# A two-layer attention and expert kernel: the first section of a group runs whole in the fourth head, and the last group's second section is cut in two

## The reference

```python
g = jax.nn.sigmoid(merge_g).reshape(B, S, N_BRANCHES, D)
mix = g[:, :, 0] * (o_sb @ w_br_sb) + g[:, :, 1] * (o_nsa @ w_br_nsa) + g[:, :, 2] * (o_moba @ w_br_moba)
x = layer_norm(DEEPNORM_ALPHA * x + mix @ w_out, ln1_g, ln1_b)
return layer_norm(DEEPNORM_ALPHA * x + peer_ffn(x, ...), ln2_g, ln2_b)

# peer_ffn, for a block of 128 tokens
v1, i1 = lax.top_k(s1, PEER_TOPK)            # scores of x @ w_q against two sets of 128 keys
v2, i2 = lax.top_k(s2, PEER_TOPK)
...
g = jax.nn.softmax(top, axis=-1)
act = jax.nn.gelu(jnp.einsum('thkd,td->thk', u_tab[idx], xb).astype(jnp.float32))
return jnp.einsum('thk,thkd->td', (g * act).astype(v_tab.dtype), v_tab[idx])
```

## Time and profile before

| | us |
|---|---|
| median of 3 runs | 2804.93 (2803.51 to 2806.49) |
| span of the profiled execution | 2819.9 |
| PE busy | 2453.4 (87%) |
| DVE busy | 1942.6 (69%) |
| POOL busy | 1233.1 (44%) |
| DMA moved | 776.98 MB, mean 276 GB/s |

### The profile page before, as it was taken

The page is one execution under the profiler, slowest core; times in us unless marked ns, Lnnn a source line. Parts: engine busy times, 40 slices in busy tenths (PEclk is TensorE's granted clock), DMA queues, the critical chain, the costliest instruction groups (busy, mean ns, idle before and its releaser), DMA issues.

```text
span 2819.9 us, 30185 instructions
## 1 busy us (share of the span) xinstructions
PE 2453.4 (87%) x10632; PEld 1484.2 (53%) x10632; DVE 1942.6 (69%) x4009; ACT 786.9 (28%) x1563; POOL 1233.1 (44%) x1028
## 2 busy tenths in 40 slices
PE   8998998998999989899988887999989999987126
PEld 4764476575445357657654465476445347644012
DVE  0122245588988875667886887587998886687875
ACT  2243222213344332321342212212445333301001
POOL 0000023354565432434553655164656352656775
PEclk9998999999989999999997998999999899999569
DMA  4323258787888776977896999787889685998998
GB/s 144 105 73 100 90 188 337 273 290 253 304 283 302 266 251 224 379 286 270 323 359 246 338 375 350 272 297 255 298 297 330 221 308 200 394 366 317 362 373 320
DMA packets 224183, 776.98 MB, mean 276 GB/s; under 512 B 23200, under 2 KB 39712, under 8 KB 219552
## 3 DMA queue, kind: packets, MB, share of 16 engines
q0 software_dynamic: 147456, 536.94, 52.1%
q1 hardware_dynamic: 73696, 227.80, 22.6%
q10 hardware_dynamic: 2880, 10.31, 0.9%
HBM read 766.56 MB, written 8.39 MB: 275 GB/s over the span
## 4 chain that ended last, share of the span: by engine, by line
PE 57%; DVE 15%; DMA 9%; issue 8%; POOL 7%; ACT 3%; another core or an unknown queue 0%; DVEq 0%; ACTq 0%; SPq 0%
PE ps L1056 14%; PE ps L931 7%; PE ps L900 6%; PE ps L984 6%; PE ps L1089 5%; POOL rows L840 4%; DVE x L1535 4%; DMA rows<-in_table_u,idx 4%; PE ps L886 3%; DMA rows<-in_table_v,idx 3%; PE ps L1124 3%; DVE rows L1520 2%; PE ps L1150 2%; DMA wring<-in_merge 2%; PE ps L993 2%
## 5 line engine op out<-in xcount | busy, mean ns | idle before, releaser
L840 POOL DMA_INDIRECT rows<-in_table_u,idx x462 | 565.2, 1223 | 1021.3 <-DVE idx L1643 506.7
L1056 PE MATMUL ps<-xT,wring 128*128 128x256 f32 x3072 | 768.1, 399 | 56.5 <-DMA wring<-in_merge 24.6
L840 POOL DMA_INDIRECT rows<-in_table_v,idx x434 | 526.5, 1213 | 490.5 <-DVE x L1535 362.4
L1056 PEld LDWEIGHTS ps<-xT,wring 128*128 128x128 f32 x3072 | 586.2, 197 | 245.4 <-issue 90.4
L1520 DVE CUSTOM_DVE_ANT_0 rows<-rows,x 128x1024 f32<-128x1024 f32 x462 | 555.0, 1223 | 120.0 <-DMA rows<-in_table_u,idx 114.3
L1535 DVE SCALAR_TENSOR_TENSOR x<-rows,wts,x 128x1024 f32<-128x1024 f32 x413 | 529.8, 1283 | 65.6 <-DMA rows<-in_table_v,idx 43.6
L1089 PE MATMUL ps<-KA,QA 33*128 33x512 f32 (+7 forms) x576 | 253.7, 537 | 26.5 <-DVE part_m L1777 12.9
L1389 ACT ACTIVATE scratch<-scratch,negm 128x640 f32<-128x640 f32 (+7 forms) x192 | 143.5, 747 | 475.3 <-DVE negm L1777 464.6
L900 PE MATMUL ps<-wring,G 128*128 128x512 f32 x384 | 184.8, 617 | 9.7 <-DVE G L1678 6.3
L1777 DVE CUSTOM_DVE_ANT_0 scratch<-ps,cst 128x128 f32<-128x128 f32 (+3 forms) x192 | 86.9, 454 | 143.0 <-PE ps L1089 140.3
L886 PE MATMUL ps<-oT,wring 128*128 128x256 f32 x384 | 126.0, 464 | 53.0 <-DVE G L1673 35.1
(11 more groups left out here) (209 smaller groups left out, 2951.4 us busy)
## 6 DMA issues: line engine op xcount, KB each, us to landing
wring<-in_merge SPq DMA_DIRECT2D x216, 512.0 KB
wring<-in_w_out_h SPq DMA_DIRECT2D x48, 512.0 KB
wring<-in_w_query SPq DMA_DIRECT2D x32, 512.0 KB
G<-in_w_query SPq DMA_DIRECT2D x12, 1024.0 KB, 8.5
G<-in_x SPq DMA_DIRECT2D x16, 512.0 KB, 4.6
G<-in_ln SPq DMA_DIRECT2D x8, 1024.0 KB, 6.8
G<-x_mid SPq DMA_DIRECT2D x16, 512.0 KB, 5.4
rows<-in_table_u,idx POOLq DMA_INDIRECT x462
```

The costliest lines, as they stand in the source:

```text
L840: pool.indirect_dma_start(row_slot(n), None, tab_u if table == "u" else tab_v, bass.IndirectOffsetOnAxis(ap=idx[:, GT * (g % 2) + t, e:e + ...
L1056: mm = pe.matmul(gate_bank(p)[:, SW * n:SW * (n + 1)], w[:, lo:lo + P], xT[:, kc, SW * (p // HALF_GATES):SW * (p // HALF_GATES + 1)], star ...
```

## The change

`SECTIONS` becomes a list of (group, tiles). The first section of every group now runs from `tanh` to `route` inside phase 3, without gates among it; gates 12 to 23 all stand in phase 4. In the last group the second section becomes two: `MIDDLE` (tile 2), placed in phase 4 behind the gates, and `LAST` (tile 3), alone behind the pass. A section of one tile has 6 merge pieces, 2 outs and 2 queries, and its merge and query matmuls move 128 columns and not 256. Both load their own weights, all through the ring.

```diff
+SECTIONS = [(g, (0, 1) if s == 0 else (2, 3)) for g in range(NG) for s in range(NS)][:-1] + [(NG - 1, (2,)), (NG - 1, (3,))]
+MIDDLE, LAST = len(SECTIONS) - 2, len(SECTIONS) - 1
 def early_section():
-    first = [("tanh", 0, 0, 0.0)] + [("gate", 0, (HALF_GATES, part), 0.0) for part in range(PARTS)]
-    first += gate_steps(HALF_GATES + 1) + [("merge", 0, k, 1.5) for k in range(12)] + section_outs(0) + gate_steps(HALF_GATES + 2)
-    second = [("norm", 0, 1, 0.0)] + gate_steps(HALF_GATES + 3)
-    second += [("turn", 0, k, 1.5) for k in range(2 * ST)] + sum([query_steps(0, k) for k in range(4)], [])
-    second += [("match", 0, k, 1.2) for k in range(2 * ST)] + [("route", 0, tt, 0.5) for tt in range(ST)]
-    return first, second + sum([gate_steps(p) for p in range(HALF_GATES + 4, GATES)], [])
+    first = [("tanh", 0, 0, 0.0)] + [("merge", 0, k, 1.5) for k in range(12)] + section_outs(0)
+    first += [("norm", 0, 1, 0.0)] + [("turn", 0, k, 1.5) for k in range(2 * ST)] + sum([query_steps(0, k) for k in range(4)], [])
+    return first + [("match", 0, k, 1.2) for k in range(2 * ST)] + [("route", 0, tt, 0.5) for tt in range(ST)]
+def tile_section(s):
+    steps = [("merge", s, k, 1.5) for k in range(6)] + section_outs(s, 1) + [("norm", s, 0, 0.0)]
+    steps += [("turn", s, k, 1.5) for k in range(2)] + sum([query_steps(s, k) for k in range(2)], [])
+    return steps + [("match", s, k, 1.2) for k in range(2)] + [("route", s, 0, 0.5)]
...
+        elif phase == 3:
+            streams.append((0.0, early_section(), 0.97))
         else:
-            streams.append((0.0, early_section()[phase - 3], 0.95))
+            own = [("tanh", MIDDLE - NS * g, 0, 0.0)] + tile_section(MIDDLE - NS * g) if g == NG - 1 else []
+            streams.append((0.0, sum([gate_steps(p) for p in range(HALF_GATES, GATES)], []) + own, 0.97))
...
-            streams.append((0.0, row_steps(phase, GT * half + phase), 0.85))
+            streams.append((0.0, row_steps(phase, GT * half + phase), 0.85 if phase < 3 else 0.5))
...
-BLOCKS = [(sec, table, ST * s + tt) for sec, (g, s) in enumerate(SECTIONS)
-          for table, tt in (("u", 0), ("u", 1), ("v", 0), ("v", 1))]
+BLOCKS = [(sec, table, t) for sec, (g, tiles) in enumerate(SECTIONS) for table in ("u", "v") for t in tiles]
...
+            def ring_section(sec):
+                for b in (2, 1, 0):
+                    load("br", sec, b)
+                if sec != MIDDLE:
+                    residual(sec)
+                for n in range(4):
+                    load("o", sec, n)
+                if sec != MIDDLE:
+                    norm_rows(sec)
+                for n in range(4, 8):
+                    load("o", sec, n)
+                for n in range(8):
+                    load("q", sec, n)
                 load("k", sec)
...
-            sp.wait_ge(oT_copied, GT * NG)
-            late_section(NS * NG - 1)
+            ring_section(MIDDLE)
+            ring_section(LAST)
```

More of the change, by code:

```diff
@@ L215, in head_steps @@
     route = [("route", -1, tt, 0.5) for tt in range(ST)]
-    steps = [("tanh", -1, 0, 0.0)]
     if g == NG:
-        steps += merge + outs + turn[0:2] + norm + turn[2:4]
-        return steps + sum(query, []) + match + route
-    steps += turns[0:2]
+        return tile_section(LAST - NS * NG)
+    steps = [("tanh", -1, 0, 0.0)] + turns[0:2]
     for n in range(6):
@@ L361, in expert_shares @@
                 late = s == 0
-            now += (.78 if kind in HEAD_KINDS or s < 0 else 1.12 if not late else 1.0 if g % 2 else 1.1) * pe
+            now += (.78 if kind in HEAD_KINDS or s < 0 else 1.12 if not late else 1.05) * pe
             if kind in ("tanh", "turn") and s < 0:
-                ahead = 1.0 if g == NG else TIGHT_AHEAD if kind == "tanh" else EXPERT_AHEAD
+                ahead = TIGHT_AHEAD if kind == "tanh" else EXPERT_AHEAD
+            if g >= NG - 1 and sec in (MIDDLE, LAST) and kind in ("merge", "turn"):
+                ahead = 0.5 if kind == "merge" or g == NG else EXPERT_AHEAD
             while nxt < ready:
@@ L683, in used @@
                     else:
-                        sp.wait_ge(done, 2 * (twos * n + m) + 2)
+                        sp.wait_ge(done, before + each * (m + 1))
             def chunks(w, lo, hi, width, h=None):
@@ L871, in section @@
             def section(sec, kind, a):
-                g, s_ = SECTIONS[sec]
+                g, tiles = SECTIONS[sec]
+                count, half, home_ = len(tiles), gate_half(sec), home_half(sec)
                 toks = section_columns(sec)
@@ L1666, in section, with own @@
-                toks = section_columns(sec)
-                if kind == "merge":
-                    k, bi, pc = 12 * sec + a, a // 4, a % 4
+                g, tiles = SECTIONS[sec]
+                count, half, home_ = len(tiles), gate_half(sec), home_half(sec)
+                if kind == "merge" and count == 1:
+                    k, bi, hf = merges_before(sec) + a, a // 2, a % 2
+                    dve.wait_ge(gate_sig, 3 * (NS * g + half) + bi + 1)
+                    dve.wait_ge(merge_done, k + 1)
+                    def own(b):
+                        return turned(b, 4 * hf, tiles[0], 4, half)
+                    v.scalar_tensor_tensor(out=own(2 - bi), in0=own(2 - bi), scalar=1.0,
+                                           in1=piece(sec, kind, a).rearrange("p (c n) -> p c n", c=4),
+                                           op0=ALU.add, op1=ALU.mult).then_inc(merged, 1)
+                    if bi > 0:
+                        dve.wait_ge(merged, k + 1)
+                        into, add = (2, 1) if bi == 1 else (0, 2)
+                        ins = v.tensor_tensor(own(into), own(into), own(add), ALU.add)
+                        if bi == 2:
+                            ins.then_inc(mixed, 1)
+                        else:
+                            after(ins)
+                            if hf == 1:
+                                v.memset(mv[:, 0, 7:8], 0.0).then_inc(x1T_free, 1)
+                elif kind == "merge":
+                    k, bi, pc = merges_before(sec) + a, a // 4, a % 4
```

317 lines of the change are left out of this document (170 added, 147 removed).

## The result

The changed kernel takes 2908.49 us (median of 4 runs, 2904.28 to 2918.66), the kernel before 2804.22 in the same session: ratio 1.0376, interval 1.035 to 1.0402. It is 3.8% slower. The forecast was 2775, its upper end 2812. The profiled execution has a span of 2902.4 us.

The account below looks back on a forecast made before the run. PE was taken as the bound up to 2457, DMA in the tail. Last route at 2583 plus 184 and 18 gave 2785; 5 to 9 added made span 2790, less 15.0 the forecast 2775 us, range 2748 to 2812.

Parts of the forecast that it names:

- Phases 3 and 4: Each group: phase 3 ends 14 us later from work moved in, phase 4 gets the rest, no cost in sum.
- The norm's wait: Phase 3: PE waits for the second tile's norm before its turns, 4.5 us a group, 18 in all.
- A wait goes: Fourth group's start: PE's 14.0 us wait for merge weights, behind SP's 20.0 us wait for a store, disappears.
- Phase 4 of the last group: With tile 2's section added, DMA is the bound: 74 MB at 400 GB/s, 185 us, 11 more than PE needs.
- The last chain: Last tile's section alone: 39.8 us of PE, 18.9 that stay and 12 for the ring, 71 us.
- The ring's 12: Last section: PE waits 12 us for weights passing through four ring slots, bounds 0 and 44.
- The second route and the norm: Last chain: 9.3 us of second route and 5.3 of norm wait were taken out of the old stretch.
- The tail: Behind the last route: 128 gathers at 1.435 us, 184 us, then 18 us to the end.
- DVE does not become the bound: In the tail DVE needs 172 us for its own rows, below the 184 of the gathers, though close.
- The second sum: DMA from row 768 on: 101 MB at 400 GB/s, 252 us to 2579, then 184 and 18, end at 2781.
- Rival (c): Phase 3: PE waits for DVE and its clock falls, 14 us more a group, end at 2830; chance 0.15.
- Rival (d): One-tile sections: narrow instructions show their weight loads, 24 us more, 2799; chance 0.04.

Follow-up runs that it names:

- E9: Changed kernel without the tanh of the four first sections, a test and no version to use: 2840.02 us, ratio 1.0122 to the kernel before.
- E3: Changed kernel with gates 12 and 13 put back behind the first section's tanh in phase 3: 2859.2 us, ratio 1.0186 to the kernel before.
- E4: Kernel before with one planner number changed, so that the third group's store of x_mid is issued sooner: ratio 1.0051 to the unedited kernel.
- E10: Changed kernel with last section unsplit, gates 12 and 13 behind the tanh, plus 20 copies of 0.5 MB in the last group's gates: ratio 1.0028 to kernel before.
- E1: Changed kernel without the split: first sections whole in phase 3, last group's second section in one piece: 2858.14 us, ratio 1.0212 to the kernel before.
- E7: Changed kernel with the third tile's route moved behind the last tile's norm on DVE: 2908.97 us, ratio 1.0271 to the kernel before.
- E8: Changed kernel with 11 expert rows fewer on DVE before the third tile's section: span 2907.0 us, ratio 1.0263 to the kernel before.

## Why the prediction was wrong

The sum of the prediction's terms ended at 2785; measured is 2902.4, 117 us more. In the median it is 133 (2908.49 for 2775): 5 us were added to the sum, and 15 were taken off because the profiled execution before lay that far above its median, while this one lies 6 below. By its own steps:

- **Phases 3 and 4, "So phase 3 ends 14 us later" and "That is no cost in sum": this step failed, 67 us.** Phase 3 grew by 32.7, 42.1, 19.2 and 41.4 us in the four groups, 135 where 4 x 14.4 + 18 = 76 were reckoned; the fifth stretch of the first three gave back 36 of the 43 expected. The step priced gates 12 and 13 as work that can stand anywhere. They were the cover of ACT's tanh, and the prediction looked only at gates 14 and 15. What stands bare once the gates are gone was asked for the norm and not for the tanh. E9 and E3 show the place; E9 also the size, 71 us in all: four waits of 8.0 us, and 46 us less of PE's busy time for the same work at a higher granted clock.
- **The norm's wait, 4.5 us a group: right.** Measured 2.9, 3.7, 4.1, 3.9.
- **"A wait goes", 14 us: right in the changed kernel.** Start to third head of the fourth group took 399.1 us for 415.6, and the four such stretches together gave back 6 more than reckoned. The reason given (rows earlier) holds, but E4 shows that it has a price elsewhere.
- **Phase 4 of the last group, 184 us: 203.7, 20 too few.** Bandwidth was taken as the only limit there. It was 350 GB/s for the assumed 400, and the stretch also has the wait of 15.1 for DVE, which stood behind rows, and of 6.8 for the norm, neither of which was in the sum.
- **The last chain, 71 us: 95.4, 24 too few.** The ring's 12 were right (9.7). The second route and the norm were struck out: the norm still stands (6.8), and the route came back in front of the next section's first merge, together with the rows before it, 19.6 us. PE's busy time was 47.8 for 39.8, at a clock of 0.76. The rest of its idle time was 11.5 for 18.9.
- **The tail, 202 us: 214.5, 12 too few.** 128 gathers is right: 881 + 15, and no row freed by PE. 1.435 us each is not: from the first at 2690.3 to the last at 2885.6 it is 195.3 / 127 = 1.54. "DVE does not become the bound": it does, where the tail starts. Two of the changed kernel's first 20 us pieces:

```profile
2708.00:2728.00 20.00, 0.00 (x0) 0.00 (x0) 19.76 (x35) 0.41 (x2) 14.53 (x12) 0.50 0.87 305
2728.00:2748.00 20.00, 0.00 (x0) 0.00 (x0) 19.86 (x37) 0.00 (x0) 16.65 (x12) 0.50 0.92 315
```

DVE has 19.8 of 20 us, PE takes no row (from 896 on come the third tile's u rows, and PE only sums v rows), DMA has room. On average over the tail DVE was below DMA, which is what the prediction compared.

These are 67 - 6 + 20 + 24 + 12 = 117 us, the whole error of the sum. The second sum, 2781, seemed to confirm the first, but it has 122 rows from 768 to 896, which are 128: 8 us more at its 400 GB/s.

Rival (c) had the right place and sign, and the cause in part: it has PE waiting for DVE and the granted clock falling, where the new wait is for ACT. It priced 14 us a group; it was 17 on average (67 / 4), and behind it came the split's cost, for which no rival stood. Rival (d) is refuted: in the third tile's section a narrow query has 128 columns and

```profile
L1011 PE MATMUL ps<-G,wring 128*128 128x128 f32 x128 | 16.8, 290 | 0.8 <-DMA wring<-in_w_query 0.8
```

16.8 / 128 = 0.131 us, near the 0.122 of the match, and under the 0.236 of the wide one. In the last tile's section, at a granted clock of 0.76, it is 0.152 (19.5 us for 128). So the prediction's reading of the Trainium skill (TensorE: Matmul & The Clock Gate, section Back-to-back issue gap) stands: the rule's ratio of 0.62 isn't what narrow float32 pieces show here. On the Trainium skill's 358 GB/s (DMA: Bandwidth & Descriptors, section Specifications) the trace now sides with the page more than with the prediction: 350 and 338 GB/s in the two stretches for which 400 was assumed, and the end would have been forecast 30 us later by it. E10's 375, each copied byte counted once, and the 400 of the earlier trace rows show that it is no hard limit here.

The second fault is in the split. The prediction never asked what the third tile's early route is for. Its row numbers matter from row 896 on and stand at 2613.4. POOL issues row 895 at 2669.2, and then:

```profile
2690.33 1.43 POOL L915 DMA_INDIRECT rows<-in_table_u,idx  x1 [20.16 <-DVE x L1616]
```

It waits 20 us for a slot, row 881's, while DVE is in the last route; that is 881 + 15 = 896. The planner's nine rows more than in E1 (881 for 872) are as many as PE frees there: in the split kernel `by_tensor` gives PE no row before 930. So E1 without the split also has 896 issued. The split's 51 us are all cost. They are 24 us more idle of PE in phase 4 (29.3 for 5.3), 27 in the last chain (47.6 for 20.6), a tail longer by 8, less 8 of busy time. Removing its waits one at a time (E7, E8) brought nothing by the stretches. Not tried: rows 881 to 895, all v rows, summed by PE during the last route of the split kernel, or another order in which the slots are there to use the early route.

## What to carry to other kernels

Work that can stand anywhere may be what covers another engine's step: before moving it, look at what stands behind the step on that engine's own list, and who needs it. Price a bare wait of PE at more than its length, by the clock behind it. And before paying for an early result, find the first instruction that could use it and what else holds that one back; a wait taken out in a stretch where gathers and DVE are near full comes back as another wait or as rows in the tail.

## What the runs showed of the hardware

In phase 3 of the first group of the changed kernel the clock was at its lower level (1.2 GHz) for 27.3 us from 221.5, in the wait of 8.0 us and behind it, and for 23.9 us more from 252.2; in E9, without that wait, the same work had 3.4 us of it. In the four groups' phase 3 the granted clock was 0.81, 0.82, 0.90 and 0.85 in the changed kernel and 0.96, 0.89, 0.95 and 0.91 in E9. It is not the same every time: E7 ran the same code with the same wait of 8.0 us at 0.72 over the 60 us where the changed kernel had 0.57, and its phase 3 took 144.2 us for 151.8. PE idled 20 us in both, so the 7.6 us of difference in one phase are the clock's.
